# A routed-expert stage turned round: token rows stationary, split fp32r weights moving, the down weights' high part cast by GpSimd

## The reference, cut to what matters

```python
for e in range(N_EXPERTS):                     # 32
    y = (silu(t @ e_gate[e]) * (t @ e_up[e])) @ e_down[e]   # t: 1024 x 1024
    out = out + combine[:, e:e + 1] * y                     # gate, up: 1024 x 256; down: 256 x 1024
```

## Time and profile before

| | |
|---|---|
| median of 3 runs | 893.04 us (891.31 to 894.35) |
| the profiled execution's own time | 892.98 us |
| its span in the trace | 891.0 us |
| TensorE / VectorE / ScalarE / GpSimd busy | 87% / 42% / 34% / 37% of the span |
| granted TensorE clock, mean | 0.941 |
| expert stage (first gate matmul to last down matmul) | 500.9 to 841.7 us |

### The profile page before, as it was taken

The page is one execution under the profiler, slowest core; times in us unless marked ns, Lnnn a source line. Parts: engine busy times, 40 slices in busy tenths (PEclk is TensorE's granted clock), DMA queues, the critical chain, the costliest instruction groups (busy, mean ns, idle before and its releaser), DMA issues.

```text
span 891.0 us, 13079 instructions
## 1 busy us (share of the span) xinstructions
PE 771.9 (87%) x5022; PEld 641.3 (72%) x5022; DVE 373.1 (42%) x767; ACT 302.0 (34%) x539; POOL 329.7 (37%) x313
## 2 busy tenths in 40 slices
PE   3999999999977888999973599999999999999700
PEld 2788888866654554787873599999998899999600
DVE  5540000046768885412238233343333333333266
ACT  6211112145558887202220233333333333333222
POOL 2432256435556771501110123443433333442134
PEclk9999999979999999999995699999999999999955
DMA  8451112000010002426358189999999999996194
GB/s 273 108 151 48 47 48 71 1 0 1 2 48 0 1 1 76 137 69 219 113 172 300 38 258 335 351 349 351 348 349 350 347 342 347 350 352 231 40 370 195
DMA packets 111238, 160.21 MB, mean 180 GB/s; under 512 B 8304, under 2 KB 88656, under 8 KB 111072
## 3 DMA queue, kind: packets, MB, share of 16 engines
q1 hardware_dynamic: 104800, 142.78, 47.9%
q0 software_dynamic: 6400, 16.92, 5.9%
HBM read 144.99 MB, written 18.87 MB: 184 GB/s over the span
## 4 chain that ended last, share of the span: by engine, by line
PE 75%; DVE 9%; ACT 6%; DMA 4%; issue 3%; POOL 1%; SPq 1%; POOLq 0%; ACTq 0%; DVEq 0%
PE ps L768 26%; PE ps L583 6%; PE ps L585 6%; PE ps L584 6%; PE ps L788 3%; PE ps L787 3%; PE ps L792 3%; PE ps L623 3%; PE ps L759 2%; PE ps L648 2%; PE ps L707 2%; PE ps L709 2%; PE ps L708 2%; PE ps L664 2%; PE ps L670 2%
## 5 line engine op out<-in xcount | busy, mean ns | idle before, releaser
L768 PEld LDWEIGHTS ps<-xT,wg 128*128 128x128 f32 x1024 | 121.6, 195 | 5.9 <-ACT xT L1016 2.3
L768 PE MATMUL ps<-xT,wg 128*128 128x96 f32 x1024 | 121.4, 278 | 1.8 <-ACT xT L1016 1.8
L768 PE MATMUL ps<-xT,wu 128*128 128x96 f32 x1024 | 119.6, 275 | 0.0
L768 PEld LDWEIGHTS ps<-xT,wu 128*128 128x128 f32 x1024 | 116.9, 192 | 0.0
L1388 DVE TENSOR_TENSOR wdlo<-wd,wdhi 128x2048 fp32r<-128x2048 f32 x32 | 73.4, 2292 | 63.0 <-ACT wdhi L1036 63.0
L583 PE MATMUL ps<-hThi,whi 128*128 128x512 f32 x224 | 88.3, 394 | 4.2 <-DVE hTlo L1086 4.2
L585 PE MATMUL ps<-hThi,wlo 128*128 128x512 f32 x224 | 87.7, 392 | 0.0
L584 PE MATMUL ps<-hTlo,whi 128*128 128x512 f32 x224 | 87.7, 391 | 0.0
L1584 POOL COPY tokc<-tok 80x1 int32 (+1 forms) x32 | 54.1, 1689 | 42.7 <-DVE tok L1369 30.7
L1597 POOL COPY destc<-dest 80x1 int32 (+1 forms) x32 | 5.7, 178 | 166.7 <-DVE ysb L1380 166.7
L1536 POOL TENSOR_SCALAR pswa<-pswa,esum 128x384 f32<-128x384 f32 (+1 forms) x48 | 55.5, 1165 | 31.8 <-DVE esum L1173 31.4
(11 more groups left out here) (194 smaller groups left out, 1415.4 us busy)
## 6 DMA issues: line engine op xcount, KB each, us to landing
wg<-in_expert_w_gate SPq DMA_DIRECT2D x32, 1024.0 KB, 8.9
wu<-in_expert_w_up SPq DMA_DIRECT2D x32, 1024.0 KB, 12.7
wd<-in_expert_w_down SPq DMA_DIRECT2D x32, 1024.0 KB, 6.0
y<-expert_rows SPq DMA_DIRECT2D x16, 512.0 KB, 9.5
wraw<-in_w_in SPq DMA_DIRECT2D x14, 512.0 KB, 3.9
xin<-in_x SPq DMA_DIRECT2D x8, 512.0 KB, 5.6
xres<-in_x SPq DMA_DIRECT2D x16, 256.0 KB, 3.0
h_rows<-h SPq DMA_DIRECT2D x8, 512.0 KB, 2.7
```

The costliest lines, as they stand in the source:

```text
L768: mm = nc.tensor.matmul(ps[:, bank, f * COLS:(f + 1) * COLS], w[:, k, c0:c0 + P], xTu[:, k, :], start=(k == 0), stop=(k == KT - 1))
```

## The change

The expert stage is rewritten. The token rows, split into `xThi` and `xTlo`, are stationary (80 columns); the weights move, 512 columns at a time (256 of gate beside 256 of up), as three fp32r products. So gate and up are 24 matmuls of 512 columns in place of 32 plain float32 matmuls of 96. Their weights must be split too: ScalarE casts the two halves of gate and up (`half_high`, 128 x 2048 each) and VectorE subtracts (`half_low`, in place). h comes out with tokens on partitions, so it is transposed (`h_rows`, 2 transposes), then split. The high part of the down weights is cast by GpSimd (`down_high`), the low part stays on VectorE. The four high-part buffers (`unit`, 8 KB a partition) are shared by the two halves and by the down weights. Gate and up are loaded as rows `(p k)`, 8 KB in one piece for each partition; the router's weights and `h2` take the same order, so `normalise2` reads with a stride of 8 elements. The copies to `tokc` and `destc` go, the row copy out is one ScalarE instruction over both banks, the hardware loops are written out, and down lies one expert behind in place of two. The overflow path is kept, with tiles of its own.

```diff
-        wdhi = [at(f"wdhi{i}", [P, 2, D], F32R, (H + 24 * KB, V)[i]) for i in range(2)]
+        unit = [at(f"unit{i}", [P, 2, 4 * DE], F32R, off) for i, off in enumerate((H + 56 * KB, H + 24 * KB, W + 56 * KB, V))]
...
+        def weight_unit(e, part):
+            return unit[(3 * e + (0, 1, 5)[part]) % 4]
+        def raw_half(w, e, a):
+            return w[e % RING][:, :, 4 * a:4 * a + 4, :].rearrange("p g k f -> p g (k f)")
...
-                return (g_src.rearrange("(k p) f -> p k f", p=P), u_src.rearrange("(k p) f -> p k f", p=P),
+                return (g_src.rearrange("(p k) f -> p k f", p=P), u_src.rearrange("(p k) f -> p k f", p=P),
...
+            def x_rows(e):
+                pe.wait_ge(xg_in[e % 2], 16 * (e // 2 + 1))
+                if e >= 1:
+                    pe.wait_ge(xThi_done, e)
+                    pe.wait_ge(xTlo_done, e)
+                rows_transposed(xg[e % 2]).then_inc(etr_done, 1)
+            def gate_up(e):
...
+                for a in range(2):
+                    hi, lo = weight_unit(e, a), raw_half(wgulo, e, a)
+                    pe.wait_ge(ahi_done, 2 * e + a + 1)
...
+                    pe.wait_ge(alo_done, 2 * e + a + 1)
...
+                    mm.then_inc(half_done, 1)
+            def h_rows(e):
+                pe.wait_ge(h_made, e + 1)
+                for j in range(2):
+                    mm = nc.tensor.transpose(ps[:, 2 + e % 2, j * COLS:(j + 1) * COLS], hx[:, j * P:(j + 1) * P], ident[0:COLS, 0:COLS])
+                mm.then_inc(htr_done, 1)
...
+            for e in range(N_EXP):
+                if e >= 1:
+                    h_rows(e - 1)
+                if e + 1 < N_EXP:
+                    x_rows(e + 1)
+                gate_up(e)
+                if e >= 1:
+                    down(e - 1)
+            h_rows(N_EXP - 1)
+            down(N_EXP - 1)
...
+            def half_high(e, a):
+                u = 3 * e + a
+                if a == 0:
+                    act.wait_ge(wgu_in[e % RING], 32 * (e // RING + 1))
+                if u >= 4:
+                    if a == 0:
+                        act.wait_ge(down_done, e - 1)
+                    else:
+                        act.wait_ge(half_done, 2 * (e - 1) + 1)
+                nc.scalar.copy(weight_unit(e, a)[:], raw_half(wgu, e, a)).then_inc(ahi_done, 1)
...
+            for e in range(N_EXP):
+                if e >= 1:
+                    h_high(e - 1)
+                if e + 1 < N_EXP:
+                    x_high(e + 1)
+                    half_high(e + 1, 0)
+                    half_high(e + 1, 1)
+                if e >= 2:
+                    rows_out(e - 2)
+                silu(e)
...
+            for e in range(N_EXP):
+                if e >= 1:
+                    h_low(e - 1)
+                if e + 1 < N_EXP:
+                    x_low(e + 1)
+                    half_low(e + 1, 0)
+                    half_low(e + 1, 1)
+                gated(e)
+                down_low(e)
...
+            def down_high(e):
+                pool.wait_ge(wd_in[e % RING], 16 * (e // RING + 1))
+                pool.wait_ge(half_done, 2 * e + 2)
+                gp.tensor_copy(weight_unit(e, 2)[:], wd[e % RING][:].rearrange("p j d -> p (j d)").rearrange("p (a f) -> p a f", a=2)
+                               ).then_inc(dhi_done, 1)
...
+            for e in range(N_EXP):
+                if e + 2 < N_EXP:
+                    gather(e + 2)
+                if e >= 2:
+                    scatter(e - 2)
+                down_high(e)
```

More of the change, by code:

```diff
@@ L521, in _ @@
             sp.wait_ge(out_mm, 2 * TT)
[L522 to L526, removed]
+            for e in range(1, N_EXP):
+                fetch_expert(e)
             sp.dma_start(gbc[:], final_g.rearrange("(a d) -> a d", a=1).partition_broadcast(P)).then_inc(g_in, 16)
@@ L811, in down_of @@
[L811 to L823, removed]
+                        nc.tensor.matmul(ps[0:CAP, b0 + n, :], hTlo_e[:, j, :], hi[:, j, n * 512:(n + 1) * 512], start=False, stop=False)
@@ new lines, in down @@
+                    if n == 0:
+                        pe.wait_ge(dlo_done, e + 1)
+                    for j in range(2):
+                        mm = nc.tensor.matmul(ps[0:CAP, b0 + n, :], hThi_e[:, j, :], wdlo[e % RING][:, j, n * 512:(n + 1) * 512],
+                                              start=False, stop=(j == 1))
+                mm.then_inc(down_done, 1)
+            pe.wait_ge(hx_zero, 1)
+            x_rows(0)
+            for e in range(N_EXP):
[6 more added lines that the diff above has]
+                    down(e - 1)
@@ new lines, in _, with v_gate_up, v_down @@
+            h_rows(N_EXP - 1)
+            down(N_EXP - 1)
+            def v_gate_up(xTu):
+                for f in range(4):
+                    c0 = (f % 2) * P
+                    for k in range(KT):
+                        mm = nc.tensor.matmul(ps[:, 2, f * COLS:(f + 1) * COLS], wgu[0][:, f // 2, k, c0:c0 + P], xTu[:, k, :],
+                                              start=(k == 0), stop=(k == KT - 1))
+                return mm
+            def v_down(hTu):
+                for n in range(2):
+                    for j in range(2):
+                        mm = nc.tensor.matmul(ps[0:CAP, 4 + n, :], hTu[:, j, 0:CAP], wd[0][:, j, n * 512:(n + 1) * 512],
+                                              start=(j == 0), stop=(j == 1))
+                return mm
@@ L1040, in y_low @@
-            def y_low(it, u):
-                e = it * RING + u
-                par = u % 2
-                act.wait_ge(down_done, e - 1)
-                if not (isinstance(it, int) and it == 0):
-                    act.wait_ge(y_put[par], put_count(it, u - 2))
-                nc.scalar.copy(ysb[par][:, 0:512], ps[0:CAP, 4 + 2 * par, :]).then_inc(y_a, 1)
-            for u in range(RING):
-                expert(0, u)
-            with act.Fori(1, N_EXP // RING) as it:
-                for u in range(RING):
-                    expert(it, u)
@@ new lines, in silu, with rows_out @@
+            def silu(e):
+                act.wait_ge(half_done, 2 * e + 2)
+                if e >= 1:
+                    act.wait_ge(h_made, e)
+                nc.scalar.activation(sg[:], ps[0:CAP, 2 + e % 2, 0:DE], ACT.Silu).then_inc(silu_done, 1)
+            def rows_out(e):
+                act.wait_ge(down_done, e + 1)
+                if e >= 2:
+                    act.wait_ge(y_put[e % 2], 16 * (e // 2))
+                b0 = 4 + 2 * (e % 2)
+                nc.scalar.copy(ysb[e % 2][:].rearrange("q (n d) -> q n d", n=2), ps[0:CAP, b0:b0 + 2, :]).then_inc(y_out, 1)
@@ new lines, in _ @@
+            act.wait_ge(tok_done, 2)
+            half_high(0, 1)
+            x_high(0)
+            for e in range(N_EXP):
+                if e >= 1:
+                    h_high(e - 1)
[3 more added lines that the diff above has]
+                    half_high(e + 1, 1)
+                if e >= 2:
+                    rows_out(e - 2)
+                silu(e)
+            h_high(N_EXP - 1)
+            rows_out(N_EXP - 2)
+            rows_out(N_EXP - 1)
@@ L1399, in _, with half_low @@
-            for u in range(RING):
-                expert(0, u)
-            with dve.Fori(1, N_EXP // RING) as it:
-                for u in range(RING):
-                    expert(it, u)
-            y_high(N_EXP // RING, 0)
-            y_high(N_EXP // RING, 1)
+            def half_low(e, a):
+                dve.wait_ge(ahi_done, 2 * e + a + 1)
+                nc.vector.tensor_tensor(raw_half(wgulo, e, a), raw_half(wgu, e, a), weight_unit(e, a)[:].bitcast(F32),
+                                        ALU.subtract).then_inc(alo_done, 1)
@@ new lines, in _ @@
+            nc.vector.memset(hx[:], 0.0).then_inc(hx_zero, 1)
+            dve.wait_ge(hx_zero, 1)
+            half_low(0, 0)
+            half_low(0, 1)
+            x_low(0)
+            for e in range(N_EXP):
+                if e >= 1:
+                    h_low(e - 1)
[5 more added lines that the diff above has]
+                down_low(e)
+            h_low(N_EXP - 1)
@@ L1612, in _ @@
+            gather(0)
+            gather(1)
+            for e in range(N_EXP):
+                if e + 2 < N_EXP:
+                    gather(e + 2)
+                if e >= 2:
+                    scatter(e - 2)
+                down_high(e)
+            scatter(N_EXP - 2)
+            scatter(N_EXP - 1)
             n_ovf = pool.value_load(eid[0:1, N_OVF:N_OVF + 1], min_val=0, max_val=N_OVF)
```

271 lines of the change are left out of this document (117 added, 154 removed).

## The result

The changed kernel takes 1133.06 us (median of 4 runs, 1132.05 to 1135.65) against 892.82 us: 1.2695 times as long, 95% interval 1.2663 to 1.2727. The forecast was 1134 us. The head of its page: span, busy times, and the chain that ended last by engine.

What follows compares the result with a forecast made beforehand. TensorE bounds the kernel before; after the change it idles in every expert. Span: 521.1 to the end of down(0), 30 periods of 18.6, 4.6 and 48.7, 1132 us; 2.0 over the span gives 1134 us; range 1080 to 1180.

Steps and rivals of the forecast that it cites:

- TensorE's own work: Expert stage: gate and up, down and transposes take 9.11 us against 10.54, 1.43 us less for each expert if nothing waits.
- The wait and the queue behind it: Expert stage: half_high waits for down(e-1), silu and gated queue behind the halves, so TensorE idles 6.9 us in every expert.
- Rival 4: Expert stage: not slower, since the wait for down(e-1) does not bind and TensorE never stops; 872 to 892 us; chance 0.05.
- The clock: Expert stage: TensorE's clock falls in each idle time, its burst starts slow; 2.3 us per expert, between 1.5 and 3.5.
- Rivals 1 and 2: Expert stage: clock survives the gaps, 16.3 us each, 1065, chance 0.07; clock never comes back, 24.6 us, 1314, chance 0.03.
- GpSimd's cast at nothing: Expert stage: down_high, 2.08 us from about 6.5 to 8.6, stays hidden as GpSimd has some 4 us of slack; cost 0.
- Rival 3: Expert stage: GpSimd's cast gets in front of VectorE, half_low ends up to 2.1 us later; 20.7 us, 1197; chance 0.05.
- The ends: Before and after the 30 periods: first gather issued 1.1 us earlier, down(0) ends at 521.1; rest behind down(31) 48.7 us.

Runs made afterwards that it cites:

- e4b_fill: Changed kernel with 28 matmuls on constants, result unused, put on TensorE behind each down to fill its gap; 1065.72 us, ratio 1.1915 to the kernel before.
- e6_gather: e1_wait with GpSimd gathering for e+3 and casting before it scatters, and silu ahead of rows_out on ScalarE; 872.40 us, ratio 0.9761 to the kernel before.
- e1_wait: Changed kernel with half_high(e, 0) waiting for down_done >= e-2 in place of e-1; 908.48 us, ratio 1.0176 to the kernel before.
- e9_keep: Changed kernel, wait kept; silu, gated and down_low ahead of the next expert's halves, GpSimd gathering for e+3 and casting before scattering; 914.76 us, ratio 1.022.
- e3_twice: Changed kernel with GpSimd making its cast of the down weights twice, down_low waiting for the second; 1138.49 us, ratio 1.2705 to the kernel before.
- e8_kp: e6_gather with the old load order (k p), pieces of 1 KB for gate and up; 892.39 us, ratio 0.9981 to the kernel before.
- e2_order: Changed kernel, wait kept; silu(e) ahead of both half_high(e+1) on ScalarE, gated(e) ahead of both half_low(e+1) on VectorE; 1051.01 us, ratio 1.1735.
- e5_load: Kernel before with only the new load order (p k) and the strided read of normalise2; 894.68 us, ratio 1.0001 to the kernel before.
- e4_fill: Changed kernel with 20 matmuls on constants, result unused, put on TensorE behind each down to fill its gap; 1108.02 us, ratio 1.2382.

## Why the prediction was right

- **TensorE's own work.** Forecast 9.11 us of work against 10.54. e4b_fill and the period of 16.2 us bear it out; and e6_gather shows that the gain is there to be had when nothing waits.
- **The wait and the queue behind it.** Forecast 6.9 us of idle time, found 6.90, with the releaser named (207.2 us in 30 waits over the stage). The terms agree within 0.2 us: the first cast ended 1.99 us after down (forecast 1.93), the second subtraction 6.51 (6.54), the product 6.84 (7.0). e1_wait (exact wait) and e9_keep (other order) each take nearly all of it away by a different edit, so the loss needs both, the wait and the order.
- **Rival 4** (the wait doesn't bind): out, by the timeline and e1_wait. Its price of 872 to 892 us was too low as well: with the exact wait alone the kernel took 908, since the gather came late, a wait that the prediction did not have; e6_gather then came to 872.
- **The clock.** Forecast 2.3 us for each expert between 1.5 and 3.5, found 2.26. Rivals 1 and 2 are out. It was a middle of two bursts read from the trace, and that the mean fell on it is partly luck; single experts vary, with periods from 17.7 to 19.5 us, one end just outside the 17.8 to 19.8 given.
- **GpSimd's cast at nothing.** Held, by e3_twice. The timing forecast was off by 0.7 us: the scatter's issue took 1.82 us in place of 0.9, so the cast ran from 714.41 to 716.31, 7.3 to 9.2 us after down, in place of 6.5 to 8.6. **Rival 3** is out in this order of things: in the changed kernel GpSimd's cast never ran when a subtraction was to start, all 96 subtractions of weights took 2.28 to 2.29 us, and where the two engines met it was GpSimd that waited. Its mechanism is real all the same: in e6_gather and e8_kp, where the cast gets to start first, a subtraction behind it takes 3.9 to 4.0 us.
- **The ends.** Two small terms were wrong, in opposite directions to a third. The first gather was to be issued 1.1 us earlier; it was, but VectorE's first subtractions, which the change puts at the same moment, stretched the issue to 2.62 us, and the first transposes came at 498.97, later than the 498.43 of the earlier trace rows:

```profile
492.71 4.49 DVE L1426 TENSOR_TENSOR wgulo<-wgu,unit 128x2048 fp32r<-128x2048 f32 x2
493.40 2.62 POOL L1647 DMA_INDIRECT xg<-h_rows,tok  x1 [31.00 <-DVE tok L1421]
...
498.97 1.51 PE L768 MATMUL ps<-ident,xg 96*128 96x96 f32 x8 [9.29 <-DMA xg<-h_rows,tok]
```

  So down(0) ended at 522.89, not 521.1. At the other end the last scatter was to come 1.24 us after down(31); it came after 1.84, since the 0.79 us that in the earlier trace rows stand in front of the scatter are there without the index copy too:

```profile
1079.35 0.61 PE L825 MATMUL ps<-wdlo,hThi_e 128*80 128x512 f32 x2
1080.00 1.01 ACT L1087 COPY ysb<-ps 80x1024 f32<-80x1024 f32 x1 [3.06 <-PE ps L825]
1081.80 0.91 POOL L1659 DMA_INDIRECT expert_rows<-ysb,dest  x1 [3.14 <-ACT ysb L1087]
```

  Against these 1.8 and 1.6 us (the rest behind down(31) was 50.3 us, not 48.7) stood 30 periods of 18.42 in place of 18.6, 5.4 us (the last of the 30, with no rows to transpose ahead, is shorter than the 29 above). That the sum came within 1 us is in part such luck.
- **Where a sum was wrong: e2_order and e1_wait.** In both, a queue was priced by its work and not read to its end: the split of h behind `down_low`, the gather behind the cast.

## What to carry to other kernels

Before you price a rewritten pipeline by engine totals, write down for each wait what is queued behind it on its engine and which engine wants the last of that first. The same over-strict semaphore count cost 225 us where the next stage's input was queued behind it (the changed kernel against e1_wait) and some 42 us where it was not (e9_keep against e6_gather). Repeated idle times on TensorE of a few microseconds can cost more than their length, since the burst behind them may start at half clock (here 2.3 us on top of 6.9); and the larger DMA pieces paid only once transfers were what was full.

## What the runs showed of the hardware

**GpSimd and VectorE hold each other up, and a GpSimd instruction that comes second waits, a DMA issue too.** That an 80 x 1 copy waits for a subtraction of two SBUF tensors was seen before; that issuing an indirect DMA does was not expected. The groups on GpSimd in the changed kernel, then the cast in e6_gather, where it meets subtractions, and the gather in e9_keep, where it meets none:

```profile
L1647 POOL DMA_INDIRECT xg<-h_rows,tok x32 | 90.4, 2826 | 39.4 <-DVE tok L1421 31.0 <-issue 5.1 <-PE ps L768 3.2
L1654 POOL CAST unit<-wd 128x2048 fp32r<-128x2048 f32 x32 | 62.0, 1939 | 13.9 <-PE ps L798 13.8
L1659 POOL DMA_INDIRECT expert_rows<-ysb,dest x32 | 57.4, 1793 | 357.2 <-ACT ysb L1087 356.9 <-issue 0.3
```

```profile
L1655 POOL CAST unit<-wd 128x2048 fp32r<-128x2048 f32 x25 | 75.1, 3003 | 18.6 <-PE ps L798 18.6
```

```profile
L1649 POOL DMA_INDIRECT xg<-h_rows,tok x22 | 21.1, 957 | 6.7 <-issue 6.7
```

The same gather takes 2.83 us and 0.96 us, the same cast 1.94 and 3.00 us. In the changed kernel a gather that starts while a subtraction runs ends 0.85 us behind that subtraction's end, a scatter 0.81 us, the cast 1.75 us: nearly their whole time alone, so hardly any of it had been done before. It goes the other way where the cast has started first. In e6_gather:

```profile
749.93 6.19 DVE L1427 TENSOR_TENSOR wgulo<-wgu,unit 128x2048 fp32r<-128x2048 f32 x2 [1.50 <-ACT unit L1051]
752.02 1.95 POOL L1655 CAST unit<-wd 128x2048 fp32r<-128x2048 f32 x1 [3.72 <-PE ps L798]
```

The second of these two subtractions starts at 752.14, 0.12 us behind the cast, and takes 3.98 us: it ends 2.15 us behind the cast, which kept its 1.95. In all 4 such meetings of e6_gather and all 7 of e8_kp the subtraction took 3.9 to 4.0 us in place of 2.29, and the earlier trace rows has a VectorE subtraction inside GpSimd's two-input ones at 1.84 us in place of 0.69. The Trainium skill, "GPSIMD Engine Reference", section "8. Key points", names the contention; by these runs the one that starts second waits. A DMA issue of GpSimd that starts first doesn't count in this: in the kernel before, 30 scatter issues had a subtraction start inside them, and both kept their times (0.94 and 2.29 us).

**A stride of 8 elements on both SBUF inputs costs VectorE.** `normalise2` over 1024 elements takes 2.22 us where it took 1.28, a price for which the trace of before had no row:

```profile
L1273 DVE SCALAR_TENSOR_TENSOR h<-x,stat,gbc 128x1024 f32<-128x1024 f32 x8 | 17.8, 2219 | 18.2 <-POOL stat L1534 18.2
```

e5_load has the same reads and shows no loss in the whole.

**A gap of about 2 us can be enough for the clock to fall, and the length of the gap alone does not decide.** Behind a gap of 2.44 us it fell in some experts of e4_fill. In e2_order it fell at about 707.2 (0.62 of full in 707 to 708), inside the gap of 1.87 us before L821 (which had one of 1.02 us shortly before it). In e9_keep it stayed full through gaps of 1.3 us in every expert, and through one of 1.97 us at 848 us.
